# Two transformer layers on one core: order of work at the networks' first steps, before the second mixer's maps, and around the per-layer input's weights

## The reference

```
x = x + 0.5*swiglu(rmsnorm(x))             # network 1, hidden width 2816
x = x + mixer1(rmsnorm(x))                 # two kinds of block attention
x = x + 0.5*swiglu(rmsnorm(x))             # network 2
x = rmsnorm(x)
# second block
proj = rmsnorm(x) @ w_in                   # 8 maps of 512 columns
x = x + [diff_attention | gated linear recurrence] @ w_out
a, u = h @ w_gate, h @ w_up                # network 3, h = rmsnorm(x)
x = x + (gelu(conv3(a) + b) * u) @ w_down
x = x + (p @ w_ple) * sigmoid(rmsnorm(x) @ w_ple_gate)   # p: 256 x 256
out = rmsnorm(x)
```

## Time and profile before

| | us |
|---|---|
| median of 3 runs | 945.37 |
| lowest, highest | 945.11, 948.29 |
| profiled execution | 945.8 |
| its span, first to last instruction | 944.0 |

### The profile page before, as it was taken

One profiled execution on the slowest core, in us unless ns is written; L12 is line 12 of the kernel. 1 busy time (PEld: TensorE's weight loads), 2 busy tenths in 40 slices (PEclk: granted clock), 3 DMA queues, 4 the chain that ended last, 5 costly groups with the idle time before them and its releaser, 6 DMA issues.

```text
span 944.0 us, 14233 instructions
## 1 busy us (share of the span) xinstructions
PE 911.4 (97%) x4869; PEld 767.9 (81%) x4869; DVE 591.0 (63%) x880; ACT 493.4 (52%) x732; POOL 113.9 (12%) x107
## 2 busy tenths in 40 slices
PE   6999999999999999999999999999999999999996
PEld 5788888887787777888888877878788999999875
DVE  5655555558856445755555567889576766667664
ACT  6544444456755546444444447656656545445463
POOL 5120000020033402000000021632002000000020
PEclk9999999999999999999999999999999999999999
DMA  9696766448722224765556536352255665555511
GB/s 310 205 274 190 221 192 208 151 124 262 239 68 87 72 65 134 224 189 188 182 187 196 188 114 223 102 179 77 67 178 176 193 199 179 182 195 173 184 45 45
DMA packets 122040, 157.43 MB, mean 167 GB/s; under 512 B 10047, under 2 KB 83011, under 8 KB 122000
## 3 DMA queue, kind: packets, MB, share of 16 engines
q1 hardware_dynamic: 119648, 151.65, 50.1%
q0 software_dynamic: 1904, 4.65, 1.9%
q10 hardware_dynamic: 448, 0.59, 0.2%
HBM read 155.79 MB, written 1.07 MB: 166 GB/s over the span
## 4 chain that ended last, share of the span: by engine, by line
PE 84%; DVE 9%; ACT 4%; issue 2%; DMA 1%; SPq 0%; DVEq 0%; ACTq 0%
PE bank L468 21%; PE bank L470 21%; PE bank L469 21%; PE bank L498 4%; PE bank L500 4%; PE bank L499 4%; DVE w_lo L1721 2%; ACT w_hi L1203 1%; PE bank L580 1%; PE bank L681 1%; PE bank L851 1%; PE bank L849 1%; PE bank L859 1%; DMA w_raw<-in_w_ffn_up 1%; DVE arena L2336 1%
## 5 line engine op out<-in xcount | busy, mean ns | idle before, releaser
L1728 DVE TENSOR_TENSOR w_lo<-w_raw,w_hi 128x1024 fp32r<-128x1024 f32 x180 | 220.2, 1224 | 177.3 <-ACT w_hi L1212 177.3
L1212 ACT ACTIVATE w_hi<-w_raw 128x1024 fp32r<-128x1024 f32 x180 | 190.2, 1058 | 210.3 <-PE bank L470 173.6
L468 PE MATMUL bank<-w_hi,x_hi 128*128 128x512 f32 (+1 forms) x680 | 274.2, 403 | 8.5 <-DVE w_lo L1721 2.6
L470 PE MATMUL bank<-w_hi,x_lo 128*128 128x512 f32 (+1 forms) x680 | 265.6, 391 | 0.0
L469 PE MATMUL bank<-w_lo,x_hi 128*128 128x512 f32 (+1 forms) x680 | 265.4, 390 | 0.0
L468 PEld LDWEIGHTS bank<-w_hi,x_hi 128*128 128x128 f32 x680 | 128.6, 189 | 42.0 <-issue 9.9
L470 PEld LDWEIGHTS bank<-w_hi,x_lo 128*128 128x128 f32 x680 | 128.8, 189 | 27.6
L1721 DVE TENSOR_TENSOR w_lo<-w_raw,w_hi 128x1024 fp32r<-128x1024 f32 x97 | 121.2, 1276 | 47.0 <-ACT w_hi L1203 46.7
L469 PEld LDWEIGHTS bank<-w_lo,x_hi 128*128 128x128 f32 x680 | 129.1, 190 | 23.7
L1203 ACT ACTIVATE w_hi<-w_raw 128x1024 fp32r<-128x1024 f32 x108 | 111.8, 1055 | 41.5 <-PE bank L470 38.2
L468 PE MATMUL bank<-w_hi,h_hi 128*128 128x512 f32 (+1 forms) x312 | 120.2, 385 | 5.8 <-DVE h_lo L1870 2.5
(11 more groups left out here) (301 smaller groups left out, 914.1 us busy)
## 6 DMA issues: line engine op xcount, KB each, us to landing
w_raw<-in_w_ffn_gate SPq DMA_DIRECT2D x132, 256.0 KB, 2.9
w_raw<-in_w_ffn_up SPq DMA_DIRECT2D x132, 256.0 KB, 3.1
w_raw<-in_w_ffn_down SPq DMA_DIRECT2D x132, 256.0 KB, 2.9
w_raw<-in_w_in SPq DMA_DIRECT2D x104, 256.0 KB, 3.1
w_raw<-in_w_out SPq DMA_DIRECT2D x32, 256.0 KB, 3.4
w_raw<-in_w_ple_gate SPq DMA_DIRECT2D x16, 256.0 KB, 3.4
arena<-bias_rows POOLq DMA_DIRECT2D x8, 256.0 KB, 4.5
w_raw<-in_cmp_w_k SPq DMA_DIRECT2D x8, 256.0 KB, 4.5
```

Of the source, the lines that this page charges most:

```text
L468: pe.matmul(out_, hi, wh, start=start, stop=False)
L470: return pe.matmul(out_, lo, wh, start=False, stop=stop)
L1212: act.activation(whi[:, slot * UNIT:(slot + 1) * UNIT], raw[:, slot * UNIT:(slot + 1) * UNIT], ACT.Copy).then_inc(sem("hi_done"), 1)
L1728: dve.tensor_tensor(wlo[:, s_], raw[:, s_], whi[:, s_].bitcast(F32), ALU.subtract).then_inc(sem("lo_done"), 1)
```

## The change

- **Second steps by banks.** `gate_up_first` replaces `gate_up(1)`: units 0 and 1 first for bank 0 alone, then for bank 1; the transposes come behind both units, where they stood behind the first.
- **Second map.** ACT splits three units and DVE two of the second mixer ahead of the statistics of its norm, where they stood behind them.
- **Opening levels.** DVE does its part of levels 2 and 3 at (3, 2), behind one remainder (L1721), where it stood behind three, at (4, 1).
- **Staging.** The copies of the seventh map (`staged2(6)`) move: on ACT ahead of the exponentials of the second head, on DVE ahead of a remainder and of `da_weights(1)`. DVE's remainder of that place goes behind the copy.
- **Per-layer units.** The first `w_ple` unit is multiplied ahead of the last down pair, the second behind it, into banks 0, 1, 6 and 7; p is transposed ahead of the last gate and up units. Transposes of `norm_chunk` for that norm go to banks 2 to 5. The first four gate units go row tile by row tile. ACT and DVE split the unit `U_GATE+2` ahead of the updates of x, and `U_GATE+3` among them.

The names at the top, and PE (the first `gate_up_first` is that of networks 1 and 2, the second that of network 3):

```diff
+U_LAST3, U_PLES = U_PLE - 1, (U_PLE - 2, U_PLE + 1)
+        PLE_BANK = {(0, 0): 0, (1, 0): 1, (0, 1): 6, (1, 1): 7}
+        def norm_bank(n, c):
+            return 2 + c if n == 5 else 6 + c % 2
...
+                def gate_up_first(between):
+                    for m in range(M):
+                        pe.wait_ge(sem("h_done"), 2 * n0 + m + 1)
+                        for j in range(2):
+                            if m == 0:
+                                pe.wait_ge(*lo_ready(base + 4 + j + 1))
+                            k_unit((base + 4 + j) % RING, j, (0, 1), tiles=(m,))
+                    gate_up_turn(1)
+                    if between:
+                        between()
+                    for j in range(2, 4):
+                        pe.wait_ge(*lo_ready(base + 4 + j + 1))
+                        k_unit((base + 4 + j) % RING, j, (0, 1))
...
+            def ple_turn():
+                pe.wait_ge(sem("p_in"), 16 * M)
+                for k in range(2):
+                    for m in range(M):
+                        mm = pe.transpose(bank[6][:, k * S + m * P:k * S + (m + 1) * P],
+                                          av(PIN + m * 256 + k * P, [P]), ident)
+                mm.then_inc(sem("pT_full"), 1)
+            def ple_unit(k):
+                u = U_PLES[k]
+                pe.wait_ge(*lo_ready(u + 1))
+                o = (u % RING) * UNIT
+                for m in range(M):
+                    for n in range(2):
+                        c = slice(o + n * 512, o + (n + 1) * 512)
+                        mm = three(bank[PLE_BANK[m, n]][:, :], xT(xhi, 4 + 2 * k + m, 1), xT(xlo, 4 + 2 * k + m, 1),
+                                   whi[:, c], wlo[:, c], k == 0, k == 1)
+                    if (k, m) == (1, 0):
+                        norm_chunk(5, 3)
+                mm.then_inc(sem("w_used"), 1)
...
+                def gate_up_first():
+                    for half in range(2):
+                        pe.wait_ge(sem("h_done"), 2 * n0 + half + 1)
+                        for j in range(2):
+                            if half == 0:
+                                pe.wait_ge(*lo_ready(base + 4 + j + 1))
+                            turned_unit((base + 4 + j) % RING, j, range(2 * half, 2 * half + 2))
+                    pe.wait_ge(sem("hlo_done"), n0)
+                    turn(True)
...
+                ple_turn()
                 gate_up(STEPS - 1)
                 down(STEPS - 1)
+                pe.wait_ge(sem("h_done"), 2 * n0 + 2 * STEPS)
+                pe.wait_ge(sem("plo_done"), 1)
+                ple_unit(0)
                 down_last(2, base, 5)
+                ple_unit(1)
...
             ffn_conv(U_FFN3)
...
-                down_unit((U_PLE + k) % RING, k, k == 0, k == 1)
-            pe.wait_ge(sem("xlo_done"), 24)
-            kblock(U_GATE, (0, 1))
-            tile_passes(U_GATE + 4, (6, 7))
+            tile_passes(U_GATE, (2, 3), ready=20)
+            tile_passes(U_GATE + 4, (4, 5))
```

On ACT:

```diff
                 conv_mid(STEPS)
+                act.wait_ge(sem("pT_full"), 1)
+                act.activation(chunk_T(xhi, 3), bank4(6), ACT.Copy).then_inc(sem("phi_done"), 1)
                 conv_gelu(STEPS)
...
+            for j in range(3):
+                split(U_IN2 + j + RING)
             stats(4, x)
...
+                    if k == 2:
+                        staged2(6)
...
             ffn_conv(U_FFN3)
+            split(U_GATE + 2)
             norm_hi(5, (0, 1))
+            split(U_GATE + 3)
+            norm_hi(5, (2,))
+            act.wait_ge(sem("w_used"), U_GATE)
+            norm_hi(5, (3,))
```

On DVE:

```diff
                 conv_taps(STEPS)
+                dve.wait_ge(sem("phi_done"), 1)
+                dve.tensor_tensor(chunk_T(xlo, 3), bank4(6), chunk_T(xhi, 3).bitcast(F32), ALU.subtract
+                                  ).then_inc(sem("plo_done"), 1)
                 conv_mul(STEPS)
...
+            for j in range(2):
+                split(U_IN2 + j + RING)
             rstd(4)
...
-                    if k in (1, 3, 5):
+                    if k == 3:
+                        staged2(6)
+                        split(U_IN2 + 26 + RING)
+                        da_weights(1)
+                    if k in (1, 5):
                         da_weights(k // 2)
...
+                    if (p, j) == (3, 2):
+                        level(2)
+                        level(3)
...
             ffn_conv(U_FFN3)
+            split(U_GATE + 2)
             update = add_ffn(2, U_FFN3, 1.0)
             update(0)
```

More of the change, by code:

```diff
@@ L584, in ffn, with gate_up_turn, gate_up @@
                 n0 = STEPS * f
-                def gate_up(i, between=None):
+                def gate_up_turn(i):
+                    if not (isinstance(i, int) and i == 1 and f == 0):
+                        pe.wait_ge(sem("hlo_done"), i + (n0 - 1))
+                    turn(False)
+                def gate_up_first(between):
[11 more added lines that the diff above has]
+                        k_unit((base + 4 + j) % RING, j, (0, 1))
+                def gate_up(i):
                     for j in range(4):
@@ L593, in gate_up @@
                         if j == 0:
[L594 to L599, removed]
+                            gate_up_turn(i)
                 def down(i, first=False, last=False):
@@ L1608, in _ @@
                             key_mix(n + 2)
-                    if j == 3:
+                    if j == 3 and p != 6:
                         staged2(p)
@@ L1666, in _ @@
             ffn_conv(U_FFN3)
+            split(U_GATE + 2)
             norm_hi(5, (0, 1))
[L1668 to L1673, removed]
+            split(U_GATE + 3)
+            norm_hi(5, (2,))
+            act.wait_ge(sem("w_used"), U_GATE)
+            norm_hi(5, (3,))
+            for j in (4, 5):
+                split(U_GATE + j)
             stats(6, x)
@@ L1677, in gate @@
             def gate(n, m):
-                act.activation(av(STG2 + 512 * (2 * n + m), [512]), bank[(0, 6)[n] + m][:, :], ACT.Sigmoid,
+                act.activation(av(STG2 + 512 * (2 * n + m), [512]), bank[2 + 2 * n + m][:, :], ACT.Sigmoid,
                                scale=sm(RSTD + m)).then_inc(sem("gate_done"), 1)
@@ L1688, in last_root @@
                 act.activation(sm(RST8 + m), sm(MS + m), ACT.Sqrt).then_inc(sem("rstd_done"), 1)
+            act.wait_ge(sem("tile0_full"), TILE0_GATE[0])
+            gate(0, 0)
             act.wait_ge(sem("w_used"), U_GATE + 4)
-            for m in range(M):
-                gate(0, m)
+            gate(0, 1)
             act.wait_ge(sem("ss_done"), 14)
@@ L2441, in _ @@
                     levels = LEVELS_AT.get((p, j), ())
-                    if (p, j) == (4, 1) or k in (1, 2):
+                    if (p, j) == (4, 1):
+                        levels = ()
+                    if k in (1, 2):
                         for n in levels:
-                            if (p, j) != (4, 1):
-                                grow_keys(n)
+                            grow_keys(n)
                         for n in levels:
@@ L2512, in _ @@
             update(3)
-            dve.wait_ge(sem("phi_done"), 1)
-            dve.tensor_tensor(hlo[:, :], bank[0][:, :], hhi[:, :].bitcast(F32), ALU.subtract).then_inc(sem("plo_done"), 1)
             scaled(5, R_PLE, 2)
+            split(U_GATE + 3)
             scaled(5, R_PLE, 3)
-            for j in range(4):
-                split(U_FFN3 + 6 * STEPS - 2 + j + RING)
+            for j in (4, 5):
+                split(U_GATE + j)
             rstd(6)
```

76 lines of the change are left out of this document (38 added, 38 removed).

## The result

The changed kernel takes 932.83 us (median of 4 runs, 932.01 to 933.19) against 946.74 of the kernel before (median of 4 runs, 945.11 to 948.29): a ratio of 0.985, interval 0.983 to 0.988. Run again among the experiments, beside 9 runs of before, it took 932.9, ratio 0.987 (0.9855 to 0.9885). The three groups of experiments have 9, 11 and 13 runs of before, with medians of 945.14, 945.04 and 945.0; against these the gain is about 12.2 us, less than the 13.9 between the first two medians. The forecast was 934.9, range 931.3 to 939.3, faster.

What follows compares the result with a forecast made beforehand. TensorE, busy 97% of the span, was taken as the bound, so only its idle time and clock losses could be won. Terms 2.2 + 0.1 + 0.7 + 0.5 + 3.65 + 3.55 = 10.7 us gave 934.9, range 931.3 to 939.3.

Steps and rivals of the forecast that it cites:

- Networks 1 and 2: First step of both networks: starting on bank 0 removes PE's waits for DVE, 1.0 and 1.2 us; gain 2.2.
- Network 3: First step: old wait of 0.9 us goes, new 0.85 wait for `h_lo` replaces it; gain 0.1, bounds 0 and 0.9.
- Second map: Second map of the mixer: earlier splits remove PE's 0.74 us wait for a remainder; gain 0.7.
- Opening levels: PE's 1.58 us wait for DVE's masked copy of level 2 goes, ACT's map 4 copies still hold PE; gain 0.5.
- the sum on DVE stays as it is: Opening levels: level 3's product, moved to 612.8, meets the same POOL instruction; if ports only shared, DVE done 0.5 us sooner.
- Staging: Ahead of the eighth map: 2.06 us wait and 1.7 us clock loss go, at most 0.2 lost; gain 3.65.
- Per-layer units: Last `down` to last matmul: 40.5 us becomes 36.9 despite new waits of 0.85 and 1.1; gain 3.55, bounds 1.9 and 5.5.
- B: Rival: new waits in network 3, at ACT at 619 and at the updates don't come; total gain 14.1, 931.3 us; chance 0.12.
- C: Rival: clock still falls at one or both places, or a new one, 1.7 us each; 936.6 or 938.3; chance 0.18.
- argument from 2.79 us of idle time: Counted against C: idle of 2.79 us, at 8 to 12 us in the span, brought no fall of the clock.
- D: Rival: single parts' gains are given back at the next joint, only the last two count; gain 7.2, 938.2 us; chance 0.09.
- E: Rival: after network 3's new wait the clock stays at 1.2 GHz through its loop; 60 us of it gives 965; chance 0.03.

Runs made afterwards that it cites:

- the changed kernel again: The changed kernel itself run once more, with nothing altered, beside runs of the kernel before: 932.9 us, ratio 0.9870.
- staging alone: The kernel before with only the staging part of the change added: 941.91 us, ratio 0.9962 to before.
- units undone: The changed kernel with the per-layer units part put back as before, all other parts kept: 935.35 us, ratio 0.9899 to before.

## Why the prediction was right, and where it was off

- **Networks 1 and 2** (2.2): right in mechanism; measured 2.45 in the pair, 2.65 undone. In network 1 the listed idle time is less than its price (1.25 listed, worth 1.5 undone), in network 2 it is not (1.24, worth 1.15). `down(1)` of network 2 did just fit, as worked out.
- **Network 3** (0.1): right in mechanism and place. The new wait was 0.53 and not 0.85: the chain from the transposes to the end of `h_lo` took 726.16 - 718.90 = 7.3 us, not the 7.6 of the earlier trace rows.
- **Second map** (0.7): right in mechanism, wrong in size. The term was the listed idle time, and was worth 1.2.
- **Opening levels** (0.5, bounds 0.2 to 1.6): the step that failed is "the sum on DVE stays as it is". The port is held as argued, but the time that DVE stands depends on which instruction meets POOL's and when; it fell from 1.24 to 0.63. The rest went as worked out: `key_mix(6)` follows the keys, ACT's two copies follow it, and PE waits 1.0 for the second of them, 1.2 us sooner than before.
- **Staging** (3.65): 3.65 in the pair, 3.7 both undone and alone, in executions with the fall.
- **Per-layer units** (3.55): 3.5 in the pair, with small errors that nearly cancel. The waits were 0.74 and 0.92 (forecast 0.85 and 1.1), 0.3 less, and the other terms took 0.5 more: from the end of the last `down` at 885.20 to that of the last matmul at 921.87 are 36.7 us, with p's transposes of 0.45 37.1, where the forecast had 36.9. What was mis-sized is the fall that went: priced at 1.7, it was worth 0.7, because the slow stretch hid a wait of 0.69. Without a fall the part is worth 2.8.
- **Rivals.** B: the new waits came, so no. C: no fall at the two places in the trace after; its argument from 2.79 us of idle time was a misreading (see the changed kernel again), the one from 1.42 stands. D: every part's gain stayed to the end. E: no.

The parts add up: 3.7 + 2.8 + 1.2 + 1.2 + 2.65 + 0.35 = 11.9 when undone one by one, and 0.7 for the clock at the end makes 12.6, against 12.4 in the pair of traces. In the total the forecast, 934.9, was 2.1 us high, of which 1.7 is too little for the parts. PE's busy time fell by 5.0 and not by 3.4: 0.8 of the difference is the clock's earlier rise at the start, which is no gain, and the rest wasn't followed up.

## What to carry to other kernels

Price an idle time at the bound engine by start-to-start times, not by the list: here 0.76 listed was worth 1.2, and 1.24 listed was worth 1.15. Before counting on a moved wait, walk the engine that releases it instruction by instruction to what comes next: three new waits were found so ahead of the run, each within 0.35 us, and the same walk then took 2.9 us more off. Where a gain is partly the clock's, compare several executions: a single trace shows a fall or its absence, not its frequency.

## What the runs showed of the hardware

**The idle time ahead doesn't decide whether the clock falls.** The idle time of 2.54 us ahead of the last pair was followed by a fall in the traces of before and of staging alone (the last row shown of it), and by none with the units undone. At 272 us three of thirteen traces fall, with no idle time over 0.05 us in the 15 us ahead, in programs that are the same up to there as others that don't. The rule in the Trainium skill, page "TensorE: Matmul & The Clock Gate", section "What's actually happening", that the gate looks at activity through a window which doesn't start with the kernel, agrees with this; no run here shows the window itself.

**How often it falls differs between the programs.** An estimate from the mean clocks: a fall of 3.4 us takes 0.0018 off the mean, and the low clock at the end of every trace, 3.2 to 5.9 us of the span, takes 0.0017 to 0.0032. So 0.997 and more is no fall, 0.996 one, 0.995 one or two, 0.994 and 0.993 two. By this all 33 executions of before and all 8 of staging alone had at least one fall, but only 2 of 6 with the units undone and 1 of 8 of the changed kernel. Why the same idle time of 2.54 us seems to bring a fall less often with the units undone stays open.

**The mean clock and the span.** The kernel before, 33 executions in the experiments' groups: mean clock 0.996, four executions, spans 941.0 to 941.8; 0.994 or 0.995, 24 executions, 941.1 to 943.9; 0.991 or 0.992, five, 944.8 to 947.0. So much of its spread goes with the clock, some 1.8 us for each step of 0.002. It is no rule for a single execution: one of the changed kernel had 0.993 and a span of 931.4, as long as another at 0.997. The mean counts the low clock behind the last matmul, which costs nothing, and leaves out the unrecorded start; which falls that execution had isn't known.

**What a fall costs depends on what stands behind it:** 1.7 us ahead of the eighth map, 0.7 at the last pair, where PE would have waited anyway.

**DVE and POOL.** The growth on POOL is listed at 1.61, 1.69 and 2.08 us, and its work was 1.15 to 1.18 in all three; the rest was DVE's instruction ahead of it.
